# Dense projections of a two-block kernel: three passes over split fp32 parts against one plain fp32 matmul

## The reference, cut to what matters

```python
# block one
proj = jnp.einsum('btd,dc->btc', xn, w_in)                                   # k, q, v, z, u: 10 units of 256 columns, and a narrow one
return jnp.einsum('btc,cd->btd', jnp.concatenate([o_delta, o_pool], axis=-1), w_out)   # 4 units
# experts: 16 x (1024x2048 gate, 1024x2048 up, 2048x1024 down), 24 MB each
# block two
proj = h @ w_in[l]                                                           # 13 units, and two narrow ones
mix = jnp.concatenate([o_a.astype(x.dtype), o_b], axis=-1) @ w_out[l]        # 4 units
x = x + (jax.nn.silu(h @ w_ffn_gate[l]) * (h @ w_ffn_up[l])) @ w_ffn_down[l] # 11 + 11 + 11 units
```

## Time and profile before

| | |
|---|---|
| median of 3 runs | 1663.29 us (1652.33 to 1664.94) |
| span of the profiled execution | 1663.7 us |
| PE busy (matmuls) | 1205.5 us, 72% |
| DVE busy | 414.8 us, 25% |
| ACT busy | 302.3 us, 18% |
| POOL busy | 318.0 us, 19% |
| moved by DMA | 479.45 MB, mean 288 GB/s |

### The profile page before, as it was taken

How to read it: one execution, slowest core, us unless ns; L and a number is a source line. 1 busy time by engine, 2 the same in 40 slices (tenths; PEclk the granted TensorE clock), 3 DMA queues, 4 the chain that set the end, 5 groups by cost and what they waited for, 6 DMA issues and landing times.

```text
span 1663.7 us, 18469 instructions
## 1 busy us (share of the span) xinstructions
PE 1205.5 (72%) x7823; PEld 721.5 (43%) x7823; DVE 414.8 (25%) x716; ACT 302.3 (18%) x399; POOL 318.0 (19%) x151
## 2 busy tenths in 40 slices
PE   5979898757556566566566556565764999789997
PEld 5978787313112112111121111111114996689996
DVE  5935344201001000000000000000007252553443
ACT  4341130100000000000000000000004344354431
POOL 4535261000000000000000000000004542545651
PEclk8979898787888788878888887878787995899999
DMA  8620015899999999999999999999994541075640
GB/s 253 232 76 1 1 29 104 347 420 415 416 421 417 416 420 418 416 419 419 416 417 420 416 416 421 416 416 421 418 402 149 155 129 49 26 240 178 202 152 26
DMA packets 136570, 479.45 MB, mean 288 GB/s; under 512 B 9138, under 2 KB 67113, under 8 KB 103625
## 3 DMA queue, kind: packets, MB, share of 16 engines
q1 hardware_dynamic: 134336, 475.12, 72.7%
q10 hardware_dynamic: 2185, 3.62, 1.3%
HBM read 476.10 MB, written 2.62 MB: 288 GB/s over the span
## 4 chain that ended last, share of the span: by engine, by line
PE 36%; DMA 31%; SPq 22%; DVE 8%; issue 1%; ACT 1%; POOL 0%; ACTq 0%; POOLq 0%; DVEq 0%
SPq L873 22%; DMA ring<-in_expert_w_gate 19%; PE bank L1020 17%; DMA ring<-in_expert_w_up 6%; DMA ring<-in_expert_w_down 5%; PE bank L1664 4%; PE bank L797 2%; DVE ring L1948 2%; PE bank L357 1%; PE bank L372 1%; PE bank L368 1%; PE bank L1204 1%; PE bank L405 1%; DVE ring L1946 1%; PE bank L403 1%
## 5 line engine op out<-in xcount | busy, mean ns | idle before, releaser
L797 PE MATMUL bank<-ring,work 128*32 128x512 f32 x2048 | 316.8, 753 | 212.0 <-DMA ring<-in_expert_w_up 132.6
L1007 POOL TENSOR_TENSOR slot_r<-ring,slot_r 128x1024 fp32r<-128x1024 f32 (+1 forms) x64 | 240.7, 3774 | 1195.5 <-ACT slot_r L996 1195.4
L797 PEld LDWEIGHTS bank<-ring,work 128*32 128x32 f32 x2048 | 62.7, 124 | 455.5 <-DMA ring<-in_expert_w_up 212.7
L813 PE MATMUL bank<-ring,work 128*32 128x512 f32 x1024 | 162.2, 767 | 104.3 <-DMA ring<-in_expert_w_down 100.0
L1020 PE MATMUL bank<-slot_r 128*128 128x256 f32 x1136 | 168.9, 296 | 11.5 <-DVE tokm_r L1426 7.2
L1020 PEld LDWEIGHTS bank<-slot_r 128*128 128x128 f32 x1136 | 158.7, 204 | 13.3 <-POOL slot_r L1007 7.4
L851 DVE TENSOR_TENSOR work<-work,bank 128x512 f32<-128x512 f32 x16 | 11.0, 687 | 508.9 <-PE bank L797 508.9
L1020 PE MATMUL bank<-work_r,slot_r 128*128 128x256 f32 x704 | 127.4, 282 | 1.6 <-DVE chan_r L1426 1.6
L813 PEld LDWEIGHTS bank<-ring,work 128*32 128x32 f32 x1024 | 31.7, 126 | 215.8 <-DMA ring<-in_expert_w_down 148.9
L858 DVE TENSOR_TENSOR hres<-hres,bank 128x512 f32<-128x512 f32 x64 | 44.0, 687 | 326.2 <-PE bank L823 326.2
L996 ACT ACTIVATE slot_r<-ring 128x2048 fp32r<-128x2048 f32 x64 | 119.7, 1902 | 8.7 <-DMA ring<-in_w_in 8.7
(11 more groups left out here) (366 smaller groups left out, 1245.7 us busy)
## 6 DMA issues: line engine op xcount, KB each, us to landing
ring<-in_expert_w_gate SPq DMA_DIRECT2D x64, 2048.0 KB, 24.0
ring<-in_expert_w_up SPq DMA_DIRECT2D x64, 2048.0 KB, 32.8
ring<-in_expert_w_down SPq DMA_DIRECT2D x64, 2048.0 KB, 32.4
ring<-in_w_in SPq DMA_DIRECT2D x23, 1024.0 KB, 7.1
ring<-in_w_ffn_gate SPq DMA_DIRECT2D x11, 1024.0 KB, 5.9
ring<-in_w_ffn_up SPq DMA_DIRECT2D x11, 1024.0 KB, 5.3
ring<-in_w_ffn_down SPq DMA_DIRECT2D x11, 1024.0 KB, 5.1
ring<-in_w_out SPq DMA_DIRECT2D x8, 1024.0 KB, 6.9
```

What stands on the lines that cost most here:

```text
L797: ins = pe.matmul(bank[b][32 * j:32 * j + 32, :], xg[:, 2 * s + kk, a * CAP:(a + 1) * CAP], ring[:, n % RING, kk * FF + j * W5:kk * FF + ( ...
L813: ins = pe.matmul(bank[YB[dh]][32 * q:32 * q + 32, :], hT[:, q * P + 32 * s:q * P + 32 * s + 32], ring[:, n % RING, q * D + dh * W5:q * D ...
L1007: eng.tensor_tensor(ring_r[s][:, at], ring[:, s, at], ring_r[s][:, at.start + UNIT:at.stop + UNIT].bitcast(F32), ALU.subtract).then_inc(S. ...
```

## The change

All splitting goes: `split_high`, `split_low`, `three`, `unit_parts`, the rounded copies of the activations and of the hidden tile, and the semaphores for them. Each product is one plain fp32 matmul on `chan` (or `qk`, `poolT`, `h_full`) and on the unit as loaded. As a unit now needs no second half, it takes half a slot: the ring holds 16 units, each half with its own semaphore (`half_in`). The ten units of block one's input projection go to halves 0 to 9 and are loaded without waiting; 13 units of block two are issued behind the last experts instead of 6, ahead of `kiwi`; the feed-forward runs 16 units ahead. Slots 0 to 3 and 5 are filled for the first expert before the output projection of block one, in place of 0, 1, 2 and 5. Some tiles of the linear attention move from `chan` to the second half of slot 6.

```diff
-                        w_ = unit_parts(pe, N_FIRST + 2 * half + i, DK)
-
+                        w_ = unit_tile(pe, N_FIRST + 2 * half + i, DK)
                         for j, k in enumerate((4, 5, 6, 7, 0, 1, 2, 3)):
-                            if t + half + i == 0 and k % 2 == 0:
-                                pe.wait_ge(S.a_lo, PIECES["mix1"] + j // 2 + 1)
-                            ins = three(pe, bank[b][:, i * UC:(i + 1) * UC], (mh1[:, k, tok], ml1[:, k, tok]),
-                                        [a[:, k, :] for a in w_], j == 0, j == DK - 1)
+                            if t + half + i == 0 and k in (0, 2):
+                                pe.wait_ge(S.odT_ready, k // 2 + 1)
+                            lhs = poolT[:, k - 4, tok] if k >= 4 else qk[:, 0, k, tok]
+                            ins = pe.matmul(bank[b][:, i * UC:(i + 1) * UC], lhs, w_[:, k, :], start=(j == 0), stop=(j == DK - 1))
...
-            freed = {0: (S.kqv_proj, 6), 1: (S.u_proj, 1), 2: (S.u_proj, 2), 3: (S.mix_out, 4), 4: (S.mix_out, 4),
+            freed = {0: (S.kqv_proj, 2), 1: (S.kqv_proj, 4), 2: (S.kqv_proj, 6), 3: (S.u_proj, 2), 4: (S.mix_out, 4),
                      5: (S.sp_out, 8), 6: (S.mix_out, 4), 7: (S.mix_out, 4)}
 
-            for n in (0, 1, 2, 5, 3, 4, 6, 7, *range(RING, PAIR * SPE)):
+            for n in (0, 1, 2, 3, 5, 4, 6, 7, *range(RING, PAIR * SPE)):
...
-        def three(pe, out_, a, b, first=True, last=True):
-
-            for i, (x_, y_) in enumerate(((a[0], b[0]), (a[0], b[1]), (a[1], b[0]))):
-                ins = pe.matmul(out_, x_, y_, start=first and i == 0, stop=last and i == 2)
-            return ins
+        def unit_tile(pe, n, k):
+            h, count = place(n)
+            pe.wait_ge(half_in[h], 16 * count)
+            return half_slot(h).rearrange("p (k c) -> p k c", k=k)
...
-            for n in range(SB_SLOTS):
-                sp.wait_ge(S.slot_used, total - RING + n + 1)
+            for n in range(SB_HALVES):
+                if n % 2 == 0:
+                    sp.wait_ge(S.slot_used, total - RING + n // 2 + 1)
                 load_unit(sp, SECOND_FIRST + n, w3[:, :, SECOND_COLS[n]:SECOND_COLS[n] + UC], DK)
             sp.wait_ge(S.slot_used, total)
-            sp.dma_start(kiwi, w3[:, :, KI:KI + 40]).then_inc(slot_in[7], 16)
+            sp.dma_start(kiwi, w3[:, :, KI:KI + 40]).then_inc(S.slot7_in, 16)
...
-                        for i, (a, b) in enumerate(((hh, wh), (hh, wl), (hl, wh))):
-                            for half in range(2):
-                                ins = pe.matmul(bank[2 * t + half][:, :], a[:, f, tok], b[:, f, half * W5:(half + 1) * W5],
-                                                start=(g == 0 and f == 0 and i == 0), stop=(last and f == FB - 1 and i == 2))
...
+                        for half in range(2):
+                            ins = pe.matmul(bank[2 * t + half][:, :], h_full(g)[:, f, t * P:(t + 1) * P], w_[:, f, half * W5:(half + 1) * W5],
+                                            start=(g == 0 and f == 0), stop=(last and f == FB - 1))
...
-                if n >= FB_SLOTS:
-                    sp.wait_ge(S.kqv_proj, n - FB_SLOTS + 1)
                 load_unit(sp, n, w_in3[:, :, c0:c0 + UC], DK)
```

More of the change, by code:

```diff
@@ L150, in sb @@
             return ctx.enter_context(nc.sbuf_tensor(name, shape, dt))
[L152 to L159, removed]
         ring = sb("ring", [P, RING, SLOT])
         hres = sb("hres", [P, TT, D])
-        chan, chan_r = sb_r("chan", [P, DK, T])
-        tokm, tokm_r = sb_r("tokm", [P, TT, D])
+        chan = sb("chan", [P, DK, T])
+        tokm = sb("tokm", [P, TT, D])
         cst = sb("cst", [P, KEEP_W])
@@ L212, in build @@
         sems("sumsq_ready root_ready rms_ready normed_ready xT_out chan_ready")
[L213 to L219, removed]
+        sems("x_in tables_in gpar_in wab_in pool_in")
+        half_in = [ctx.enter_context(nc.semaphore(f"half_in{s}")) for s in range(2 * RING)]
         def vec(name, i=0, n=None):
@@ L809, in experts_pe @@
                         n = SPE * a + 8 + s
[L810 removed]
+                        sem, count = expert_in(n)
+                        pe.wait_ge(sem, 48 * i + count)
                         for dh in range(2):
@@ L974, in place @@
             if n < N_FIRST:
-                return n % FB_SLOTS, landed(n % FB_SLOTS, "first", n // FB_SLOTS + 1)
+                return n, 1
             if n < SECOND_FIRST:
-                s = MIX1_SLOTS[n - N_FIRST]
-                return s, landed(s, "mix1")
+                return MIX1_HALVES[n - N_FIRST], 2 if MIX1_HALVES[n - N_FIRST] < N_FIRST else 1
+            earlier = [mixer_loads(h) + (0 if h % 2 else SPE * N_EXPERTS // RING) for h in range(2 * RING)]
             m = n - SECOND_FIRST
@@ L980, in place @@
             if m < N_SECOND:
-                return m % SB_SLOTS, landed(m % SB_SLOTS, "second", m // SB_SLOTS + 1)
+                h = m % SB_HALVES
+                return h, earlier[h] + m // SB_HALVES + 1
             m = n - FF_FIRST
-            s = FF_SLOTS[m % RING]
-            return s, landed(s, "ffn", m // RING + 1)
-        def load_unit(sp, n, src, k):
-            s, _ = place(n)
-            sp.dma_start(ring[:, s, 0:UNIT].rearrange("p (k c) -> p k c", k=k), src).then_inc(slot_in[s], 16)
@@ L993, in split_high @@
[L993 to L1007, removed]
-                              ALU.subtract).then_inc(S.w_lo_dve if on_dve else S.w_lo_pool, 1)
@@ new lines, in place, with mixer_loads, expert_in, half_slot @@
+            return h, earlier[h] + (h < SB_HALVES) + (h + SB_HALVES < N_SECOND) + m // len(FF_HALVES) + 1
+        def mixer_loads(h):
+            return int(h < N_FIRST) + int(h in MIX1_HALVES)
+        def expert_in(n):
+            h = 2 * (n % RING)
+            return half_in[h], 16 * (mixer_loads(h) + n // RING + 1)
+        def half_slot(h):
+            return ring[:, h // 2, (h % 2) * UNIT:(h % 2 + 1) * UNIT]
+        def load_unit(sp, n, src, k):
+            h, _ = place(n)
+            sp.dma_start(half_slot(h).rearrange("p (k c) -> p k c", k=k), src).then_inc(half_in[h], 16)
@@ L1395, in second_pool @@
                     pool.wait_ge(S.mask_ready, u // 8 + 1)
-                    pool.wait_ge(slot_in[7], landed(7, "second", 3))
+                    pool.wait_ge(S.slot7_in, 48)
                 if u >= 2:
@@ L2063, in _ @@
                 for i in range(2):
-                    w_ = unit_parts(pe, 8 + i, DK)
+                    w_ = unit_tile(pe, 8 + i, DK)
                     for k in range(DK):
-                        ins = three(pe, bank[ZB[t]][:, i * UC:(i + 1) * UC], (xh1[:, k, tok], xl1[:, k, tok]),
-                                    [a[:, k, :] for a in w_], k == 0, k == DK - 1)
+                        ins = pe.matmul(bank[ZB[t]][:, i * UC:(i + 1) * UC], chan[:, k, tok], w_[:, k, :],
+                                        start=(k == 0), stop=(k == DK - 1))
                 ins.then_inc(S.z_proj, 1)
```

259 lines of the change are left out of this document (70 added, 189 removed).

## The result

The changed kernel took 1697.59 us, the median of four runs (1691.86 to 1698.77), beside 1663.95 us for the kernel before (four runs, 1652.33 to 1664.94). The ratio is 1.0218, with a 95% interval of 1.0171 to 1.0265: slower by 34 us. Forecast were 1703 us and slower.

A forecast was written before the change was run, and what follows sets the result against it. Taken as bounds: TensorE and VectorE before the experts, weight loads in them, mostly TensorE after. Terms -9.9 + 1.8 + 0 + 6.0 + 41.8 = +39.7 us on a span of 1663.7 gave 1703 us, range 1690 to 1716.

The forecast's parts named there:

- The price of a product: TensorE, all units: 0.4325 us per plain product of 256 columns, 0.86 of 512; each unit costs 1.1 to 1.3 us more.
- Rival 2: TensorE: a plain product costs four of today's passes, 0.472 us, a unit 7.55; 1744 us in all; chance 0.06.
- rival 1: TensorE: the plain product is as cheap as three passes, so all released time counts; 1627 us; chance 0.03.
- Feed-forward: Dense feed-forward, 33 units: eleven groups of 20.72 us in place of 16.92, +41.8 us, nothing given back.
- Block one's projections: Start to end of z part: earlier first product and faster convolutions without splits, -9.9 us, bounds -6.5 to -12.5.
- Block one's output projection: Before it, splits and waits go, -3.3 us; its 64 products take +5.1; together +1.8 us.
- Experts: 0: Expert weight stream: 184 slots of 5.04 us, 928.1 us, unchanged; a shift of what comes before passes through whole.
- The fifth slot: Ring before the experts: one more slot filled early brings nothing, as all eight are full before first use; otherwise -5.0 us.
- rival 4: Front gives more: clock stays high through block one and the extra early-filled slot counts, 2.6 + 5; 1695 us; chance 0.13.
- Block two: From last expert slot to feed-forward: start 7.2 us earlier, dearer products, fewer splits; sum +6.0 us.
- kiwi: Small load behind block two's 13 units on SP: lands a microsecond or two after them, four microseconds of cover, nothing added.
- rival 3: Block two: the small load queued behind 13 units is late, TensorE waits 4 to 5 us; 1709 us; chance 0.10.

The follow-up runs named there:

- fifth_slot_late: Changed kernel with ring slot 3 filled only after block one's output projection, so four expert slots are filled early, not five: 1694.53 us.
- three_pass_no_low: Kernel before, three passes kept, without low parts of block one's ten input units (high part read twice; not the reference's result): 1637.57 us, ratio 0.9878.
- block_one_plain_norm_first: Kernel before with plain products in block one alone, and GpSimd delaying block two's first splits until the norm's squares are summed: 1646.45 us, ratio 0.9927.
- block_one_plain: Kernel before with plain fp32 products in block one alone, whole slots kept: 1651.53 us, ratio 0.995.
- gpsimd_busy: Changed kernel with eleven unused subtractions added on GpSimd beside block one's convolutions: 1706.79 us, ratio 1.0296.

## Why the prediction was right, point by point

**The price of a product** held: 0.4316 us against the 0.4325 read off eight products in the earlier trace rows, and 6.87 / 8 = 0.859 against the 0.86 of the earlier trace rows. These two short stretches of the kernel before were enough. Rival 2, with four of today's passes (0.472), falls, and so does rival 1, which wanted a unit under 6.3 us and got 6.9. The Trainium skill, FP8 and Floating Point Precision, TensorE Precision Notes, counts four passes for true fp32: a pass of the plain product is then 0.4316 / 4 = 0.108 us, and one of the three that it replaces is 11.32 / 96 = 0.118 us. The count of passes agrees with these traces, but the passes are not equal, and 4/3 overstates the step.

**Feed-forward**, forecast +41.8: +41.4 in the groups (11 x 3.76), +40.0 from the start of the feed-forward to the end of the span. The difference of 1.4 us was not in the sum: the first two groups' gate and up units lost 1.5 us to the low clock before (24.17 where two times 11.32 would be 22.64) and 0.7 after (28.32 where two times 13.81 would be 27.62), and what stands behind the last product was 0.6 us shorter.

**Block one's projections**, forecast -9.9: -10.4, z ends at 102.85 against 103.3. That it fits to half a microsecond is luck: two terms erred and cancel, and other traces with the same plain front end z between 99.4 and 106.0 us. The eight units end at 76.76, not 74.8: TensorE starts at 16.07, and the 192 records behind L1870 take 43.19 us, where 0.4316 each would make 41.4. The granted clock was 0.90 in the first 16.4 us after those narrow matmuls, which the forecast had charged to the z part and not here. In `fifth_slot_late` the same six units took 41.54 us, so this loss belongs to the execution. And the step to the z part took 5.9 us, not 8.7: the forecast had priced its narrow matmuls from rows at the low clock. Convolutions: 7.94 us against 7.9 foretold.

**Block one's output projection**, forecast -3.3 and +5.1: -5.2 and +5.0. The excess of 2 us in the first lies in the second scan of the delta rule, where TensorE came back from the low clock earlier. The two traces of `three_pass_no_low` show this stretch to move by 3.6 us in one and the same program, so that none of the 2 us can be called a gain of the change.

**Experts: 0**, forecast and measured (928.15 and 928.17 us). The shift went through whole. The fifth slot was foretold at nothing, and two experiments found nothing. That is what separates the forecast from rival 4 (1695 us, by a high clock and by this slot), which the time of 1697.59 alone doesn't: rival 4's 5 us of the slot are not there.

**Block two**, forecast +6.0: +2.7. The start came 6.9 us earlier (7.2 foretold). Behind it, the stretch of the thirteen units grew by 12.8 us and not by 14.4, `w_out_2` by 3.4 (28.24 for 24.82) and not by 4.9, the stretch between them shrank by 5.8 and not by 4.6, and the last one, before the feed-forward, by 0.7 and not by 1.5. The term that was most mis-sized is the "+2" for the low clock at `w_out_2`: 64 products at 0.4316 would take 27.6 us and took 28.24, so it was 0.6. In the first three units likewise, 22.64 us for a foretold 23.6. Of the 5.8 us, 1.7 are attention at a little more of the clock, which `block_one_plain_norm_first` has as well with three passes in block two.

**`kiwi`** was foretold to land in time with 4 us of cover. The timeline of POOL, the kernel after:

```profile
1273.83 1.43 POOL L1305 COPY work<-ring 128x256 f32<-128x256 f32 x4 [1062.84 <-DMA ring<-in_w_in]
```

It had landed by 1273.8, 40.1 us behind the start of the last slot's matmuls; foretold were 39.2 for the thirteen units and one or two more for `kiwi`. The copies took 1.43 us and not 3.42, with no split beside them, and TensorE wanted them at 1281.42: 6 us of cover, and rival 3 falls.

**The sum** was 7.5 us too high on the span (39.7 against 32.2): 3.3 in block two, 2.4 in block one, 1.8 in the feed-forward and the tail. These are misses in size and not in mechanism, and together they stay inside the range of 1690 to 1716.

## What to carry to other kernels

Price an alternative instruction from the nearest place where the kernel already issues it, and multiply: that settled the sign here, because TensorE alone made the chain in the part that grew most. When a change removes work from engines that are off the chain, the gain is only where that work stood in somebody's way; look for instructions that take many times their own duration, and first try to move what disturbs them, as one added wait gave 6 us here where three passes stayed. Try the parts of a change apart: here one was worth half a per cent and another cost two. And look at every single time before you compare two medians: where runs lie in two groups, as those of `block_one_plain` do, the median says which group had more runs.

## What the runs showed of the hardware that was not expected

- Beside GpSimd's subtractions of 3.70 us, VectorE's `scalar_tensor_tensor` of 128x256 took 3.75 us each in place of 0.425 (`gpsimd_busy`, the first four). GpSimd's four small copies took 3.42 us before, where VectorE's splits overlapped them, and 1.43 after: it seems that both sides pay, though no run tested this second direction by itself.
- By the four passes cited above, a plain fp32 matmul comes out cheaper per pass than an fp32r one: 0.108 against 0.118 us for 256 columns, 0.859 / 4 = 0.215 against 5.60 / 24 = 0.233 for 512.
- The granted clock of one stretch can differ between two executions of one program (1.00 and 0.72, worth 3.6 us). Attention was found at 0.84 and at 0.50, worth some 10 us on the same instructions, for a cause that these runs don't show.
